# Twelve key/value cache copies: seven move from ScalarE's queue to the end of SyncE's queue

## The reference, cut to what it computes

```python
def layer(x, ple, conv_buf, h0, pos, attend, lw):
    h = rmsnorm(x, lw['g_mix'])
    z = h @ lw['w_in']                      # 1024 x 8704
    ...                                     # conv, RG-LRU; q, k with norm and rotary
    att, kv_new = attend(q, k, v)           # three groups of heads
    b_att = att @ lw['w_br_att']
    merged = jax.nn.sigmoid(g_lru) * b_lru + jax.nn.sigmoid(g_att) * b_att
    x = x + merged @ lw['w_out']
    x = x + moe(rmsnorm(x, lw['g_ffn']), ...)   # top 4 of 32 experts, 1024 x 2048 and 1024 x 1024 each
    x = x + jax.nn.sigmoid(rmsnorm(x, lw['g_ple']) @ lw['w_ple_gate']) * (ple @ lw['w_ple'])
    return x, kv_new, conv_new, h_new

# in attend_sample, for each group (cache of 128, 512 or 1024 positions, 4 KB a position):
k_all = jnp.concatenate([cache[:, :, 0], k], axis=1)
news.append(jnp.stack([k_all[:, -wb:], v_all[:, -wb:]], axis=2))
```

## Time and profile before

| | us |
|---|---|
| median of 3 runs (lowest, highest) | 1526.54 (1523.99, 1527.29) |
| the profiled execution, whole | 1525.43 |
| its span | 1523.6 |
| outside the span | 1.83 |

### The profile page before, as it was taken

One profiled execution on the slowest core, in us unless ns is written; L12 is line 12 of the kernel. 1 busy time (PEld: TensorE's weight loads), 2 busy tenths in 40 slices (PEclk: granted clock), 3 DMA queues, 4 the chain that ended last, 5 costly groups with the idle time before them and its releaser, 6 DMA issues.

```text
span 1523.6 us, 16360 instructions
## 1 busy us (share of the span) xinstructions
PE 1385.3 (91%) x6726; PEld 710.0 (47%) x6726; DVE 392.4 (26%) x527; ACT 200.0 (13%) x343; POOL 18.5 (1%) x31
## 2 busy tenths in 40 slices
PE   7999997968898899999999999999999999999848
PEld 5887885854776433333333333333333333333227
DVE  2015943172223122212212121122122122121123
ACT  1113110241300210110110101101101101100001
POOL 0000000030000000000000000000000000000000
PEclk9999998989997899999999999999999999999979
DMA  9687999263555789999999999999999999999910
GB/s 386 265 350 245 336 345 367 103 203 131 198 236 208 269 358 429 428 428 428 429 428 427 429 429 427 428 428 430 427 427 429 429 428 428 429 429 427 427 49 29
DMA packets 39918, 530.42 MB, mean 348 GB/s; under 512 B 5839, under 2 KB 5983, under 8 KB 10535
## 3 DMA queue, kind: packets, MB, share of 16 engines
q1 hardware_dynamic: 36834, 470.65, 74.5%
q10 hardware_dynamic: 1685, 54.43, 9.1%
q0 software_dynamic: 1360, 4.76, 1.3%
HBM read 525.07 MB, written 58.38 MB: 383 GB/s over the span
## 4 chain that ended last, share of the span: by engine, by line
PE 47%; DMA 46%; DVE 3%; issue 2%; ACT 1%; another core or an unknown queue 0%; SPq 0%; DVEq 0%; ACTq 0%
DMA ring<-in_wexp 42%; PE PS L719 16%; PE PS L489 12%; DMA ring<-in_win 4%; PE PS L647 3%; PE PS L858 2%; PE PS L665 2%; PE PS L628 1%; PE PS L765 1%; PE PS L500 1%; PE PS L532 1%; PE PS L734 1%; DVE ring L1153 1%; PE PS L596 1%; PE PS L680 1%
## 5 line engine op out<-in xcount | busy, mean ns | idle before, releaser
L719 PE MATMUL PS<-ring,Zb 128*64 128x512 f32 x3072 | 690.7, 600 | 42.5 <-DMA ring<-in_wexp 39.3
L719 PEld LDWEIGHTS PS<-ring,Zb 128*64 128x64 f32 x3072 | 211.7, 137 | 472.3 <-issue 374.4
L489 PE MATMUL PS<-hT,ring 128*128 128x264 f32 x1024 | 232.3, 390 | 12.4 <-DMA ring<-in_win 12.4
L489 PEld LDWEIGHTS PS<-hT,ring 128*128 128x128 f32 x1024 | 196.9, 193 | 47.4 <-issue 13.2
L1355 DVE COPY Zb<-PS 64x512 f32<-64x512 f32 x32 | 21.9, 683 | 319.4 <-PE PS L719 319.4
L1019 ACT ACTIVATE Zb<-Zb 128x512 f32<-128x512 f32 x32 | 20.1, 629 | 449.4 <-DVE Zb L1333 449.4
L765 PE MATMUL PS<-Zb 128*128 128x264 f32 x256 | 74.1, 412 | 3.9 <-DVE xc L1323 2.4
L1323 DVE TENSOR_TENSOR xc<-xc,PS 128x528 f32<-128x528 f32 x68 | 47.6, 700 | 107.3 <-PE PS L765 100.4
L765 PEld LDWEIGHTS PS<-Zb 128*128 128x128 f32 x256 | 43.4, 189 | 58.8 <-issue 48.7
L1011 ACT ACTIVATE Zb<-PS 128x512 f32<-128x512 f32 x32 | 19.1, 597 | 367.4 <-PE PS L748 367.4
L734 PE MATMUL PS<-Zb 128*64 128x512 f32 x256 | 62.5, 610 | 1.4 <-DVE Zb L1288 1.4
(11 more groups left out here) (221 smaller groups left out, 843.6 us busy)
## 6 DMA issues: line engine op xcount, KB each, us to landing
ring<-in_wexp SPq DMA_DIRECT2D x192, 2048.0 KB, 24.4
ring<-in_win SPq DMA_DIRECT2D x17, 2048.0 KB, 15.1
out_kvs<-in_cache ACTq DMA_DIRECT2D x8, 4032.0 KB, 25.3
out_kvs<-in_cache ACTq DMA_DIRECT2D x8, 1984.0 KB, 12.7
ring<-in_kt SPq DMA_DIRECT2D x2, 2048.0 KB, 15.0
ring<-in_cache SPq DMA_DIRECT2D x2, 2048.0 KB, 9.1
ring<-in_w_br_lru SPq DMA_DIRECT2D x2, 2048.0 KB, 14.3
ring<-in_w_out SPq DMA_DIRECT2D x2, 2048.0 KB, 14.1
```

The source lines that it names most:

```text
L489: last = mm(PS[:, t, 0:T], w[:, k, t * P:(t + 1) * P], hT[:, k, :], start=(k == 0), stop=(k == KT - 1))
L719: last = mm(PS[CAP * h:CAP * (h + 1), bank, :], src[:, k, f:f + CAP], w[:, k, h * CH:(h + 1) * CH], start=(not seeded and slot % 2 == 0 an ...
```

## The change

`EARLY` goes from 6 to 4, so that ACT issues streams 0 to 3 of the third group at pieces 8 to 11 and none at pieces 12 and 13. Streams 4 to 7 and the three `shift_rest` are issued by SP, directly behind the two halves of w_ple_gate and ahead of the two output stores. The two helper functions become common to both engines. Bytes copied, their shapes and the semaphore that counts them are the same.

```diff
-EARLY = 6
+EARLY = 4
...
+        def shift(eng, g, b):
+
+            n = (WB[g] - 1) // 16 * 16
+            eng.dma_start(a[f"kvs{g}"][b, 0:n, :].rearrange("(q r) n -> q (r n)", q=16),
+                          a[f"cache{g}"][b, 1:n + 1, :].rearrange("(q r) n -> q (r n)", q=16)).then_inc(S.kv_copy, 16)
+
+        def shift_rest(eng, g):
+
+            n = (WB[g] - 1) // 16 * 16
+            eng.dma_start(a[f"kvs{g}"][:, n:WB[g] - 1, :].rearrange("b r n -> r b n"),
+                          a[f"cache{g}"][:, n + 1:WB[g], :].rearrange("b r n -> r b n")).then_inc(S.kv_copy, 16)
...
             sp.wait_ge(S.g1_mm, E)
             half(a["w_ple_gate"], 0, wpg[0], S.wpg_in)
             half(a["w_ple_gate"], 4, wpg[1], S.wpg_in)
+            for b in range(EARLY, NS):
+                shift(sp, 2, b)
+            for g in range(NG):
+                shift_rest(sp, g)
             for half_ in range(2):
...
             with act.Fori(LOOP_A, LOOP_A + EARLY) as i:
                 for t in range(4):
                     evac(4 * i + t, t)
-                shift(2, i - LOOP_A)
+                shift(act, 2, i - LOOP_A)
             with act.Fori(LOOP_A + EARLY, NPIECE) as i:
                 for t in range(4):
                     evac(4 * i + t, t)
...
             root(2, rstd[:, :], PS[:, 0, 0:T], 1.0 / D).then_inc(S.rms_ok, 1)
 
-            for b in range(EARLY, NS):
-                shift(2, b)
-            for g in range(NG):
-                shift_rest(g)
             for b, (t0, nt) in enumerate(BLK):
```

More of the change, by code:

```diff
@@ L885, in evac @@
                 A(Z[:, n, :], PS[:, bank, 0:T], ACT.Copy).then_inc(S.z_evac, 1)
[L889 to L900, removed]
+            shift(act, 0, 0)
+            shift(act, 1, 0)
             act.wait_ge(S.z_evac, 4)
@@ L904, in _ @@
                     evac(4 * i + t, t)
-                shift(0, i)
-                shift(1, i)
+                shift(act, 0, i)
+                shift(act, 1, i)
             for c in range(13):
```

## The result

The changed kernel is slightly slower: 1530.18 us (median of 20 runs) against 1526.87 (median of 20), ratio 1.0020 with an interval of 1.0011 to 1.0028. The prediction was 1522.0 us, 4.5 us faster than before: the measured time lies inside its range of 1510 to 1538, but on the other side of the kernel before. The profiled execution took 1531.18 us, its span is 1529.4 (before 1523.6).

The account below looks back on a forecast made before the run. Transfers bound the experts, whose stretch moves as a block; PE's load waits in w_in and jumps in the tail were open to change. 1525.43 - 16.5 - 0 + 0 + 12 = 1520.9, on the median's scale 1522.0; range 1510 to 1538.

Parts of the forecast that it names:

- Part 1: w_in stage: without streams 4 and 5 at pieces 12 and 13, PE's waits for pieces 14 and 15 go, minus 16.5 us.
- Part 2: Ahead of the experts: five copies leave ACT, but the expert loads start no earlier, 0 us (bounds 0 to 1 gain).
- Part 3: Tail: seven copies on SP behind w_ple_gate take about 50 us under other work and cost 0 us as transfers.
- the cover: Tail: the copies end by 1511 and the last store is issued by 1520.6, so 9 us are spare.
- Part 4: PE's jumps before the last product: instruction packets wait behind the copies' parts, plus 12 us (bounds 5.5 to 19.3).
- the high bound: PE's jumps in the tail: every one of seven packets waits a whole part, 7 x 2.75 = 19.3 us.
- the rhythm: PE's jumps: first packet waits 1.4 us; three later rounds wait 0.7 plus 2.75 each; 11.8 in all, called 12.
- 2.4 us per packet: PE's jumps in the tail: the wait for each of seven packets at which the 16.5 us gain is used up.
- the middle value: PE's jumps in the tail: 12 us, taken between the bounds of 5.5 and 19.3 us.

Follow-up runs that it names:

- part 3 alone: The changed kernel with EARLY = 6: streams 4 and 5 stay at pieces 12 and 13, streams 6, 7 and leftover rows behind w_ple_gate on SP; 1532.62 us, ratio 1.0050.

## Why the prediction was wrong

- **Part 1, minus 16.5 us: right.** 16.0 us in the profile, 16.3 in the run without the tail's copies. Piece 14's load landed at 228.9 and PE waited 0.3 us for it; the later loads were there in time, piece 15's at 233.8. Less the 1.7 us of the late start these are 227.2 and 232.1, within 0.7 us of the forecast. The size of the gain is known to some 2 us: two other profiled executions with streams 4 and 5 at pieces 12 and 13 (part 3 alone, and the kernel before without jumps) take 1.7 and 2.4 us less from the place at 130 us to the gates than the kernel before did.
- **Part 2, 0 us: not contradicted.** The run without tail copies gains what part 1 alone explains. No run isolates it closer than its own spread.
- **Part 3, the transfers themselves, 0 us: right, with the cover thinner than worked out.** They landed at 1499.7, 27 us ahead of the last store; they took 54 us and not 50. Without the long idle time of PE they are the end, as the kernels without jumps and with one jump show.
- **Part 4, plus 12 us: this step failed.** The mechanism was named rightly and is shown by three runs that vary it in different ways (no copies, no jumps, eight free engines). The term was mis-sized: 19.8 us were measured, just above the high bound that the prediction had worked out, 7 x 2.75 = 19.3, for every packet waiting a whole part. That the two agree is luck: by the same bound, parts of 4 KB would cost 7 x 0.2 = 1.4 us, and they cost 12.1. The step that was wrong is the rhythm, by which a packet asked for 2.0 us into a part would wait only 0.7. It takes for granted that an engine holds one part at a time. The packets' places in the profile say otherwise: the first is under way at the earliest 5 us after PE stops, some 4 later than before, where the rhythm has a wait of 1.4; and with parts of 4 KB, where the rhythm would give nearly nothing, 1.7 us per packet stay.
- **The sum.** 16.0 gained and 19.8 lost give plus 3.8; measured plus 3.3. The prediction said itself that 2.4 us per packet decide; it was 2.8. The forecast hung on a term known only from 5.5 to 19.3 us against a gain of 16.5, and the middle value was chosen by a picture of the queue that no row bore out. That is where the chance of 0.55 for faster was too high.
- **The rule of the Trainium skill** (DMA: Bandwidth & Descriptors, Queues, rings and completion order) that an engine drains a packet of some 9 to 17 descriptors before it changes queues: with parts of 4 KB the wait of 1.7 us is about nine parts of 0.2 us, which is near it; with parts of 64 KB such a turn would be above 20 us, and the wait is 2.8. The measurement decides: not a fixed number of descriptors. The Trainium skill's rule that a taken branch out of the present window forces a fetch by DMA (Runtime: NRT & Kernel Launch, Instruction fetch mechanics) agrees with the trace: without the jumps the 18.3 us shrink to 3.2.

## What to carry to other kernels

Idle DMA engines are not free where an engine jumps over code: its instructions come through the same engines, and each packet waits behind what stands there. Before filling an idle stretch with transfers, look in it for "issue" gaps with packets in the instruction queue, and first make the jumps few, by nesting guards. Where a bulk copy shares engines with loads that someone waits for, cut the copy into smaller parts than the loads before moving it: here that alone gave the full 16 us.

## What was not expected of the hardware

- SP is held while it issues copies of many small parts into a full queue. SP's own rows in the kernel with 4 KB parts in the tail: four copies take 47.5 us to issue (2.55 with 64 KB parts), and with 8 engines 69.9.

```profile
1421.55 47.52 SPq L349 DMA_DIRECT2D out_kvs<-in_cache  x4
1469.11 13.87 SPq L355 DMA_DIRECT2D out_kvs<-in_cache  x3
```

  It cost nothing here, as SP's next duty was at 1504.8. With 8 engines it did: the output stores waited for it until 1514.7.
- Part size changed who waits, not the throughput: streams in 4 KB parts move at 332 GB/s in 1450 to 1478, those in 64 KB parts at 328.
- A request that meets full engines waits even when the parts ahead of it are tiny: a load's first part at least 3.2 us with parts of 4 KB, against less than 1 us on idle engines, and an instruction packet 1.7 us on the average of seven.
